# Pairs on diagonal strips, updates on two row strips, and the samples' queries as stationary column strips

## The chip, the cores and the metric

The kernel runs on one core of one Trainium2 chip. The metric is the device time of one execution in microseconds (us), as the median of several runs.

## The reference

One step of a recurrent decoder trunk: 256 prompt tokens and 8 samples of 4 tokens, 288 in all, width 2048. One normalised input goes through a large projection to five branches, each with its own gate; each branch is projected back, weighted by a sigmoid gate from the same input, summed and projected once more. Two branches are of one kind, and the change touches them alone: HGRN2 (8 heads, keys 128, values 128) and GLA (4 heads, keys 128, values 256). Per head, with a running sum b of log decays in chunks of 64 tokens:

```python
b = jnp.cumsum(gi, axis=2)
inter = jnp.einsum("nhtk,nhkv->nhtv", qi * jnp.exp(b), S)
decay = jnp.where(mask, jnp.exp(jnp.where(mask, diff, 0.0)), 0.0)
att = jnp.einsum("nhtk,nhsk,nhtsk->nhts", qi, ki, decay)
intra = jnp.einsum("nhts,nhsv->nhtv", att, vi)
S_new = jnp.exp(b_last)[..., None] * S + jnp.einsum("nhsk,nhsv->nhkv", ki * jnp.exp(b_last[:, :, None] - b), vi)
```

The prompt starts from a zero state; each of the 8 samples has a state S of its own per head, loaded from HBM, used by its 4 tokens and written back renewed.

## The kernel before

Weights stream in 522 units of 512 KB through four slots. SyncE issues each load when the slot's last unit was split; ACT rounds a unit to `w_hi` (fp32r), DVE subtracts to get `w_lo`, and PE does three matmuls per 128x128 block (hi*hi, lo*hi, hi*lo), 288 columns of tokens each, in `project`. A projection from the model width has two units and 48 matmuls, a branch's own projection (`branch`) one unit and 24. The order of all this is written out by hand: the list `ORDER`, and on ACT and DVE calls `upto(n)`, which process the units up to n in the engine's own queue. All work between the projections stands in the same queues. Each engine runs its list in order.

The stages touched run from about 560 to 1400 us: four GLA heads, then eight HGRN heads. The attention matrix of 128 tokens is built by levels: `HALVES` 64, 32, 16, ..., 1. For level l the distances of the decay to the middle of each block of 2h tokens stand in `g_X[:, l]`; after the exponentials on ACT (`distances`) DVE multiplies them with queries in the right half and keys in the left (`keys_and_queries`). Then PE multiplies `g_X[:, l]` with itself over 128 tokens (`pairs`), once for each level and once keys by queries for the diagonal, into two banks of PSUM (2 and 3). DVE masks the eight slices (`levels`) and sums them (`attention`). This is done for tokens 0 to 127 in `first_pairs`, for 128 to 255 in `second_pairs`, which waits for DVE to free the banks, a projection later. `first_pairs` also makes the samples' own 32x32 products (three, as only levels 2 and 1 and the diagonal lie within 4 tokens), the product between the two halves of the prompt, and the turned keys (`g_kT`). `end_keys_and_queries` gives the queries times exp(b) in the slot `CROSS` and signals `g_X`.

`mixed` sums, for a block of 128 values: attention times values, and for each of the 8 samples the whole state (128x128) as stationary operand with that sample's 4 query columns moving. `updates` makes what is added to the samples' states: turned keys of the 32 sample tokens (`g_kT[0:TS, 2]`) times the values, laid out by DVE (`own_values`) so that each sample has columns of its own, two products of 512 columns into banks 5 and 6; `new_states` adds them. GLA calls it twice a head (half 0 and 1), HGRN once, after the next head's forget projection and its `sum_squares`.

PE's order in an HGRN head is: hf, sum_squares and updates of the head before, hq, hi, gate C, turn_values, hg, first_pairs, gate C, second_pairs, two branch projections, mixed. In a GLA head: decay product, ck, cq, cv, cv, turn_values, gate D, first_pairs, cg, second_pairs, cg, mixed (values 0), branch, mixed (values 1), gate, updates, branch, sum_squares, gate, updates, and the rest of the gates and branches. GpSimd loads a head's states (`g_S0_landed`) when the stores of the head before have ended. The memory attention (`kc`, `eq_own`) and the S5 branch already use 32-wide strips of PE's array: an output on 32 partitions at 32j, with a stationary operand of 32 columns.

## Time and profile before

| | us |
|---|---|
| median of 3 runs | 2012.35 (2010.4 to 2014.06) |
| the profiled execution | 2009.41 |
| its span | 2007.7 |
| PE busy | 1949.1 |
| DVE busy | 1275.2 |
| ACT busy | 903.4 |
| POOL (GpSimd) busy | 414.1 |
| mean granted TensorE clock | 0.992 |

The span is the time from the first to the last instruction in one execution taken by the hardware profiler. PE is the matmul part of TensorE; an instruction's duration there is from its start to the end of its results, and consecutive ones overlap, so distances between starts say what one costs. One fp32 product shows as two matmul records, an fp32r one or a transpose as one. All helpers of one kind have one line (L1615 for matmuls), so groups are told apart by the names of their tiles. "ps" is PSUM.

### The profile page before, as it was taken

To read this page: it belongs to the slowest core of one execution; us is meant where nothing else is said; L and a number is where in the kernel's file an instruction comes from. 1 tells how busy PE (TensorE), PEld (TensorE's weight loads), DVE (VectorE), ACT (ScalarE), POOL (GpSimd) and SP (SyncE) were. 2 spreads that over 40 slices of the span, in tenths; PEclk is the share of its full clock that TensorE was granted. 3 is DMA by queue.
4 is the path that set the end of the run, shared out by engine and by line. 5 is a ranking of instruction groups with operands and counts; after the bars stand their busy time and mean duration, and the time that the engine had idled before them with its cause. 6 is when DMAs were issued, how large, how long until landed. Compare 5 with 4: busy or idle time off the path is not lost.

```text
span 2007.7 us, 37182 instructions
## 1 busy us (share of the span) xinstructions
PE 1949.1 (97%) x15518; PEld 1875.7 (93%) x15518; DVE 1275.2 (64%) x2106; ACT 903.4 (45%) x1307; POOL 414.1 (21%) x704
## 2 busy tenths in 40 slices
PE   6999999999999999999999999999999999999996
PEld 5999998999999999999999999999999999999996
DVE  8555467776575766666778777777565565544544
ACT  5543444544444344435455555454333333434442
POOL 5687778787000000000000000000000000000000
PEclk9999999999999999999999999999999999999998
DMA  7777664445444353535434344444555444454542
GB/s 269 279 280 257 236 216 163 168 171 182 164 155 174 136 180 126 186 122 185 146 138 170 130 157 138 149 148 144 205 186 191 170 154 156 171 198 158 177 160 90
DMA packets 91512, 350.50 MB, mean 175 GB/s; under 512 B 11760, under 2 KB 12160, under 8 KB 87760
## 3 DMA queue, kind: packets, MB, share of 16 engines
q1 hardware_dynamic: 76896, 280.53, 40.6%
q0 software_dynamic: 11568, 47.50, 6.6%
q10 hardware_dynamic: 2880, 20.09, 2.6%
q8 instruction: 123, 2.02, 0.4%
q14 instruction: 45, 0.37, 0.1%
HBM read 321.15 MB, written 26.92 MB: 173 GB/s over the span
## 4 chain that ended last, share of the span: by engine, by line
PE 59%; DVE 7%; ACT 4%; issue 3%; DMA 0%; POOL 0%; ACTq 0%; DVEq 0%
PE ps L1615 58%; DVE w_lo L1041 2%; DVE g_X L1035 2%; DVE g_X L1041 1%; ACT g_t L569 1%; ACT L569 1%; ACT w_hi L569 1%; DVE g_X L1044 0%; ACT g_X L569 0%; DVE g_b L1470 0%; PE ps L1922 0%; DVE acc L1038 0%; DMA a_h<-in_a_h 0%; DVE acc L1035 0%; DVE g_k L1041 0%
## 5 line engine op out<-in xcount | busy, mean ns | idle before, releaser
L1615 PE MATMUL ps<-h_hi,w_hi 128*128 128x288 f32 x2960 | 890.8, 301 | 18.7 <-ACT gate_t L569 7.3
L1041 DVE TENSOR_TENSOR w_lo<-raw,w_hi 128x1024 fp32r<-128x1024 f32 x522 | 650.8, 1258 | 393.3 <-ACT w_hi L569 389.9
L1615 PE MATMUL ps<-h_hi,w_lo 128*128 128x288 f32 x2960 | 877.1, 296 | 0.0
L1615 PE MATMUL ps<-h_lo,w_hi 128*128 128x288 f32 x2960 | 872.5, 295 | 3.0 <-DVE h_lo L1041 3.0
L569 ACT ACTIVATE w_hi<-raw 128x1024 fp32r<-128x1024 f32 x522 | 546.5, 1055 | 540.7 <-PE ps L1615 523.2
L1615 PEld LDWEIGHTS ps<-h_hi,w_hi 128*128 128x128 f32 x2960 | 559.3, 189 | 36.1 <-issue 17.8
L1615 PEld LDWEIGHTS ps<-h_lo,w_hi 128*128 128x128 f32 x2960 | 559.8, 189 | 3.6 <-DVE h_lo L1041 3.6
L1615 PEld LDWEIGHTS ps<-h_hi,w_lo 128*128 128x128 f32 x2960 | 560.2, 189 | 0.8
L1615 PE MATMUL ps<-br_hi,w_hi 128*128 128x288 f32 x640 | 193.1, 302 | 1.6 <-DVE d_gate L1047 1.6
L1615 PE MATMUL ps<-br_lo,w_hi 128*128 128x288 f32 x640 | 189.7, 296 | 0.0
L1615 PE MATMUL ps<-br_hi,w_lo 128*128 128x288 f32 x640 | 189.5, 296 | 0.0
L1615 PEld LDWEIGHTS ps<-br_hi,w_hi 128*128 128x128 f32 x640 | 120.9, 189 | 10.3 <-issue 7.3
L1615 PEld LDWEIGHTS ps<-br_hi,w_lo 128*128 128x128 f32 x640 | 120.4, 188 | 0.1
L1615 PEld LDWEIGHTS ps<-br_lo,w_hi 128*128 128x128 f32 x640 | 120.1, 188 | 0.0
L569 ACT ACT_TABLE_LOAD x85 | 109.1, 1283 | 4.9 <-PE ps L1615 2.6
L344 POOL DMA_DIRECT2D out_hg_s<-h_S x8 | 4.3, 532 | 439.1 <-DVE h_S L1047 439.1
L569 ACT ACTIVATE gate_t<-ps 128x288 f32<-128x288 f32 x80 | 32.3, 404 | 137.6 <-PE ps L1615 137.3
L1615 PE MATMUL ps<-o_hi,w_lo 128*128 128x288 f32 x256 | 76.6, 299 | 0.0
L1615 PE MATMUL ps<-o_lo,w_hi 128*128 128x288 f32 x256 | 76.1, 297 | 0.0
L1615 PE MATMUL ps<-o_hi,w_hi 128*128 128x288 f32 x256 | 75.7, 296 | 0.0
L344 POOL DMA_DIRECT2D out_gla_s<-c_S x4 | 2.1, 534 | 356.3 <-DVE c_S L1047 356.3
L1615 PE MATMUL ps<-m_hi,w_hi 128*128 128x256 f32 x256 | 72.3, 283 | 0.5 <-DVE gate_t L1047 0.3
(371 smaller groups left out, 2409.4 us busy)
## 6 DMA issues: line engine op xcount, KB each, us to landing
raw<-in_w SPq DMA_DIRECT2D x522, 512.0 KB, 3.8
w_scratch<-st_wide POOLq DMA_DIRECT2D x72, 128.0 KB, 3.5
a_w<-w_scratch POOLq DMA_DIRECT2D x8, 1152.0 KB, 8.1
acc<-in_kc ACTq DMA_DIRECT2D x4, 2048.0 KB, 7.9
vc<-in_vc ACTq DMA_DIRECT2D x4, 2048.0 KB, 10.1
c_S<-in_gla POOLq DMA_DIRECT2D x4, 1024.0 KB, 7.2
out_gla_s<-c_S POOLq DMA_DIRECT2D x4, 1024.0 KB, 5.1
h_S<-in_hgrn POOLq DMA_DIRECT2D x8, 512.0 KB, 3.9
```

The costliest lines, as they stand in the source:

```text
L344: pool.dma_start(dst, src).then_inc(S(name), 16)
L569: act.activation(out, in_, func, **kw).then_inc(sem if not isinstance(sem, str) else S(sem), 1)
L1035: return dve.tensor_tensor(out, a, b, ALU.mult)
L1041: return dve.tensor_tensor(out, a, b, ALU.subtract)
L1615: return pe.matmul(out, a, b, start=start, stop=stop)
```

## The change

- Pairs: for levels 16 to 1 and the diagonal only the 32x32 blocks on the diagonal of the 128 tokens are multiplied, four blocks on four column strips (bank 2); levels 64 and 32 multiply only the blocks that are not masked, four products ("far", bank 3). Both halves of the prompt are done in one `all_pairs`; `second_pairs` goes.
- Samples' states: the 4 queries of each sample stand in 32 columns of a cleared tile `g_own` and are the stationary operand on a column strip; the state moves through (`ps[:, 7]`, in `all_pairs`). ACT copies the results to `of_states`; `mixed` adds them by two products of 16 columns with columns of the identity. The wait for the loaded states moves from `mixed` to `all_pairs`.
- Updates: samples 0 to 3 stay on rows 0 to 15, samples 4 to 7 get rows 64 to 79; the two products of 512 columns have 16 rows each on two row strips. For this the keys and values of samples 4 to 7 are turned by an added product with the identity each and copied by ACT.
- DVE's `attention` masks and sums 2 x 192 columns, spreads the sums over the strips and copies the far blocks. Masks are prepared on GpSimd.

```diff
-        g_vm = g_prod[0:TS].rearrange("p l t -> p (l t)")
+        g_vm = g_prod[:].rearrange("p l t -> p (l t)")[:, 0:512]
+
+        def of_states(nv):
+
+            return g_prod[:].rearrange("p l t -> p (l t)")[:, 512:512 + 2 * nv * P].rearrange("p (h c) -> p h c", h=2)
+
+        halves_of_samples = (slice(0, 16), slice(64, 80))
+        g_own = sb("g_own", [P, NB, 32], F32, g_st)
...
+        near = levels[:, 1058:1250].rearrange("p (l t) -> p l t", t=32)
+        strips = levels[:, 1250:1254]
+        in_strip = levels[:, 1254:1258]
+        in_strip2 = levels[:, 1258:1262]
...
-            for mask, width, pattern in ((in_group[:], 16, [[-16, 8]]), (in_half[:, 0], 64, [[-64, 2]]),
-                                         (in_seq[:], NT, [[-NT, NB]])):
+            for mask, width, pattern, first in ((in_group[:], 16, [[-16, 8]], 0), (in_half[:, 0], 64, [[-64, 2]], 0),
+                                                (in_strip, NT, [[-NT, 4]], 0), (in_strip2, NT, [[-NT, 4]], 64)):
                 link(pool.memset(mask, 1.0))
-                for base, sign in ((0, 1), (width - 1, -1)):
...
+            by_strip = lev_mask[:, 2:8, :].rearrange("p l (s t) -> p l s t", s=4)
+            link(tt(ALU.add, near, by_strip[:, :, 0], by_strip[:, :, 1]))
+            for n in (2, 3):
+                link(tt(ALU.add, near, near, by_strip[:, :, n]))
+            link(tt(ALU.add, in_strip, in_strip, in_strip2))
+            link(tt(ALU.add, strips, in_group[:, 0:8:2], in_group[:, 1:8:2]))
             link(pool.memset(eq_own[:], 0.0))
...
+            pool.memset(g_own[:], 0.0).then_inc(S("g_own_clear"), 1)
...
+                f(vals[2][64:80, 2], ps[64:80, 4, 0:nv * P], ACT.Copy, "g_vT")
...
+                f(of_states(nv), ps[:, 7, 0:2 * nv * P].rearrange("p (h c) -> p h c", h=2), ACT.Copy, "g_of_states")
                 f(g_kT[:, 0:2], ps[:, 5, 0:2 * P].rearrange("p (a b) -> p a b", a=2), ACT.Copy, "g_kT")
                 f(g_kT[0:TS, 2], ps[0:TS, 5, 2 * P:3 * P], ACT.Copy, "g_kT")
+                f(g_kT[64:80, 2], ps[64:80, 5, 2 * P:3 * P], ACT.Copy, "g_kT")
...
-                mul(cross[:, P:T], cross[:, P:T], g_q[:, P:T])
+                mul(cross[:, P:SEQ], cross[:, P:SEQ], g_q[:, P:SEQ])
+                dve.wait_ge(S("g_own_clear"), 1)
+                mul(g_own[:, :, 0:NT], by_seq(cross), by_seq(g_q))
                 sg(mul(final, final, g_k[:]), "g_X")

-            def attention(i, nv, n):
+            def attention(i, nv):
                 w, _ = heads_of(i, nv)
-                w("levels", 3, 1 + 2 * n)
-                link(mul(g_prod[:].rearrange("p l t -> p (l t)"), ps[:, 2:4].rearrange("p a t -> p (a t)"),
-                         levels[:, 0:1024]))
-                sg(dve.tensor_reduce(g_att[:, 2 * n], g_prod[:].rearrange("p l t -> p t l"), AX.X, ALU.add), "g_att")
-                w("att", 3, 1 + 2 * n)
-                if n == 0:
-                    w("levels", 3, 2)
-                    own = g_prod[0:TS, 0:3, 0:TS]
-                    link(mul(own, ps[0:TS, 4, 0:3 * TS].rearrange("p (l t) -> p l t", t=TS), lev_mask[0:TS, 5:8, 0:TS]))
-                    sg(dve.tensor_reduce(g_atts[:], own.rearrange("p l t -> p t l"), AX.X, ALU.add), "g_att")
-                    w("att", 3, 2)
+                w("levels")
+                flat = g_prod[:].rearrange("p l t -> p (l t)")
+                prod = flat[:, 0:384].rearrange("p (a l t) -> p a l t", a=2, l=6)
+                summed = flat[:, 384:448].rearrange("p (a t) -> p a t", a=2)
+                own = flat[0:TS, 0:96].rearrange("p (l t) -> p l t", t=TS)
+                far = ps[:, 3, 0:SEQ].rearrange("p (a t) -> p a t", a=2)
+                att = g_att[:, 0:3:2]
+                for a in range(2):
+                    ins = mul(prod[:, a], ps[:, 2, 192 * a:192 * a + 192].rearrange("p (l t) -> p l t", t=32), near)
+                link(ins)
+                link(dve.tensor_reduce(summed, prod.rearrange("p a l t -> p a t l"), AX.X, ALU.add))
+                for a in range(2):
+                    ins = mul(att[:, a].rearrange("p (s t) -> p s t", s=4), summed[:, a:a + 1].to_broadcast([P, 4, 32]),
+                              strips.unsqueeze(2).to_broadcast([P, 4, 32]))
+                link(ins)
+                link(mul(own, ps[0:TS, 4, 0:3 * TS].rearrange("p (l t) -> p l t", t=TS), near[0:TS, 3:6]))
+                dve.tensor_reduce(g_atts[:], own.rearrange("p l t -> p t l"), AX.X, ALU.add)
+                for rows, cols in ((slice(0, 64), slice(64, 128)), (slice(0, 32), slice(32, 64)), (slice(64, 96), slice(96, 128))):
+                    ins = dve.tensor_copy(att[rows, :, cols], far[rows, :, cols])
+                sg(ins, "g_att")
+                w("att")
...
             def own_values(i, nv, vals, half):
                 w, wv = heads_of(i, nv)
-                n = NB // nv
+                n = 4 // nv
                 if half:
                     wv("up", half)
                 else:
-                    w("vT", 3, 3)
-                sg(mul(g_vm.rearrange("p (b v) -> p b v", v=nv * P),
-                       vals[2][0:TS, 2].unsqueeze(1).to_broadcast([TS, n, nv * P]),
-                       in_seq[:, half * n:(half + 1) * n].unsqueeze(2).to_broadcast([TS, n, nv * P])), "g_vm")
+                    w("vT", 4, 4)
+                for rows in halves_of_samples:
+                    ins = mul(g_vm[rows].rearrange("p (b v) -> p b v", v=nv * P),
+                              vals[2][rows, 2].unsqueeze(1).to_broadcast([16, n, nv * P]),
+                              in_strip[rows, half * n:(half + 1) * n].unsqueeze(2).to_broadcast([16, n, nv * P]))
+                sg(ins, "g_vm")
...
                     w("o")
-                for b in range(n):
-                    s = vals[0][:, half * n + b]
-                    ins = stt(s, s, g_eb[:, half * n + b:half * n + b + 1], up[:, b * nv * P:(b + 1) * nv * P],
-                              ALU.mult, ALU.add)
+                for j in range(2):
+                    for b in range(n):
+                        of = 4 * j + half * n + b
+                        s = vals[0][:, of]
+                        ins = stt(s, s, g_eb[:, of:of + 1], ps[:, 5 + j, b * nv * P:(b + 1) * nv * P], ALU.mult, ALU.add)
                 sg(ins, "g_new" if half == nv - 1 else "g_half_new")
...
-                attention(i, 2, 0)
+                attention(i, 2)
-                attention(i, 2, 1)
...
-                attention(i, 1, 0)
-                upto(u0 + 13)
-                attention(i, 1, 1)
+                attention(i, 1)
...
                         pe.transpose(ps[:, 2 + tt, v * P:(v + 1) * P], vals[1][:, v, tt * P:(tt + 1) * P], ident[:])
-                    ins = pe.transpose(ps[0:TS, 4, v * P:(v + 1) * P], vals[1][:, v, SEQ:T], ident[:])
+                    pe.transpose(ps[0:TS, 4, v * P:(v + 1) * P], vals[1][:, v, SEQ:T], ident[:])
+                for v in range(nv):
+                    ins = mm(ps[64:80, 4, v * P:(v + 1) * P], vals[1][:, v, SEQ + 16:T], ident[:])
                 sg(ins, "g_vt")

-            lev = ps[:, 2:4].rearrange("p a (l t) -> p (a l) t", t=P)
-
             def pairs(tok):
-                for l in range(7):
-                    mm(lev[:, l], g_X[:, l, tok], g_X[:, l, tok])
-                sg(mm(lev[:, DIAG], g_k[:, tok], g_q[:, tok]), "g_levels")
-
-            def first_pairs(i, nv):
+
+                at_ = tok // P * 192
+                for n in range(6):
+                    for j in range(4):
+                        c = slice(tok + 32 * j, tok + 32 * j + 32)
+                        x, y = (g_X[:, n + 2, c], g_X[:, n + 2, c]) if n < 5 else (g_k[:, c], g_q[:, c])
+                        mm(ps[32 * j:32 * j + 32, 2, at_ + 32 * n:at_ + 32 * n + 32], x, y)
+
+                for l, j, first, width in ((0, 0, 64, 64), (0, 1, 64, 64), (1, 0, 32, 32), (1, 2, 96, 32)):
+                    mm(ps[32 * j:32 * j + 32, 3, tok + first:tok + first + width],
+                       g_X[:, l, tok + 32 * j:tok + 32 * j + 32], g_X[:, l, tok + first:tok + first + width])
+
+            def all_pairs(i, nv, vals):
                 w, _ = heads_of(i, nv)
                 w("X")
-                w("vT", 3, 3)
-                pairs(slice(0, P))
+                w("vT", 4, 4)
+                pairs(0)
+                pairs(P)
+                n, _ = heads_before(i, nv)
+                pe.wait_ge(S("g_S0_landed"), n * 16 + 16)
+                for half in range(2):
+                    for j in range(4):
+                        b = 4 * half + j
+                        mm(ps[32 * j:32 * j + 32, 7, half * nv * P:(half + 1) * nv * P], g_own[:, b], vals[0][:, b])
                 for n, (a, b) in enumerate(((g_X[:, 5], g_X[:, 5]), (g_X[:, 6], g_X[:, 6]), (g_k, g_q))):
                     ins = mm(ps[0:TS, 4, n * TS:(n + 1) * TS], a[:, SEQ:T], b[:, SEQ:T])
                 sg(ins, "g_levels")
                 mm(ps[:, 6, 0:P], g_X[:, CROSS, 0:P], g_X[:, CROSS, P:2 * P])
                 for tt in range(2):
                     pe.transpose(ps[:, 5, tt * P:(tt + 1) * P], g_X[:, FINAL, tt * P:(tt + 1) * P], ident[:])
-                sg(pe.transpose(ps[0:TS, 5, 2 * P:3 * P], g_X[:, FINAL, SEQ:T], ident[:]), "g_kt")
-
-            def second_pairs(i, nv):
-                w, _ = heads_of(i, nv)
-                w("att", 3, 1)
-                pairs(slice(P, 2 * P))
+                pe.transpose(ps[0:TS, 5, 2 * P:3 * P], g_X[:, FINAL, SEQ:T], ident[:])
+                sg(mm(ps[64:80, 5, 2 * P:3 * P], g_X[:, FINAL, SEQ + 16:T], ident[:]), "g_kt")

             def mixed(i, nv, vals, v):
                 w, _ = heads_of(i, nv)
-                n, _ = heads_before(i, nv)
                 if v == 0:
-                    w("att", 3, 3)
+                    w("att")
                     w("cross_out")
-                    pe.wait_ge(S("g_S0_landed"), n * 16 + 16)
+                    w("of_states")
+                own = ident[:].rearrange("p (j r) -> p j r", r=32)[:, :, 0:NT]
                 out, val = ps[:, 2 + v], lambda m: vals[2][:, m, v * P:(v + 1) * P]
                 mm(out[:, 0:2 * P], val(0), g_att[:, 0:2].rearrange("p a t -> p (a t)"), True, False)
                 mm(out[:, P:2 * P], val(1), g_att[:, 2], False, False)
                 mm(out[:, SEQ:T], val(2)[0:TS], g_atts[:], False, False)
-                for b in range(NB):
-                    seq = slice(SEQ + b * NT, SEQ + (b + 1) * NT)
-                    ins = mm(out[:, seq], vals[0][:, b, v * P:(v + 1) * P], g_X[:, CROSS, seq], False, b == NB - 1)
+                for half in range(2):
+                    ins = mm(out[:, SEQ + 16 * half:SEQ + 16 * half + 16], of_states(nv)[:, half, v * P:(v + 1) * P], own,
+                             False, half == 1)
...
-                w("kT", 2, 2)
+                w("kT", 3, 3)
...
                 wv("vm", half + 1)
                 if half:
                     pe.wait_ge(S("g_half_new"), i + 1)
-                mm(ps[:, 5], g_kT[0:TS, 2], g_vm[:, 0:512])
-                sg(mm(ps[:, 6], g_kT[0:TS, 2], g_vm[:, 512:1024]), "g_up")
+                for j, rows in enumerate(halves_of_samples):
+                    ins = mm(ps[:, 5 + j], g_kT[rows, 2], g_vm[rows])
+                sg(ins, "g_up")
...
-                first_pairs(i, 2)
+                all_pairs(i, 2, c_values)
                 h("cg", 2 * i)
-                second_pairs(i, 2)
...
-                first_pairs(i, 1)
+                all_pairs(i, 1, h_values)
                 gate("C", 2 * i + 1)
-                second_pairs(i, 1)
```

## Rows read from the trace of the kernel before

**Rows 1.** The page, part 1: busy us by engine, share of span, instructions

```profile
PE 1949.1 (97%) x15518; PEld 1875.7 (93%) x15518; DVE 1275.2 (64%) x2106; ACT 903.4 (45%) x1307; POOL 414.1 (21%) x704
```

**Rows 2.** Who PE waited for: total us, times, longest us

```profile
PE ps L1615 <- DVE w_lo L1041: 4.3, 8, 0.6
PE ps L1615 <- DVE g_X L1035: 3.1, 7, 0.5
```

**Rows 3.** PE, third HGRN head: start us, duration us, instruction, count [idle before]

```profile
1079.55 1.83 PE L1615 MATMUL ps<-g_X 128*128 128x128 f32 x14 [0.44 <-DVE g_X L1035]
1081.53 0.31 PE L1615 MATMUL ps<-g_X 128*32 128x32 f32 x4
1081.68 0.23 PE L1615 MATMUL ps<-g_q,g_k 128*32 128x32 f32 x2
1081.84 0.49 PE L1615 MATMUL ps<-g_X 128*128 128x128 f32 x2
1082.41 0.38 PE L1615 MATMUL ps<-h_hi,w_hi 128*128 128x288 f32 x1
```

**Rows 4.** The same view, the second block of pairs of that head

```profile
1088.89 1.77 PE L1615 MATMUL ps<-g_X 128*128 128x128 f32 x14
1090.64 0.38 PE L1615 MATMUL ps<-br_hi,w_hi 128*128 128x288 f32 x1
```

**Rows 5.** PE timeline with four column strips: memory attention, S5 branch

```profile
72.09 1.93 PE L1615 MATMUL ps<-acc,eq_own 128*32 128x256 f32 x32
73.95 0.38 PE L1615 MATMUL ps<-m_hi,w_hi 128*128 128x256 f32 x1
...
1401.88 0.64 PE L1615 MATMUL ps<-a_w 128*32 128x128 f32 x16
1402.45 0.40 PE L1615 MATMUL ps<-h_hi,w_hi 128*128 128x288 f32 x1
...
1429.99 1.21 PE L1615 MATMUL ps<-a_H,a_w 128*32 128x72 f32 x64
1431.13 0.40 PE L1615 MATMUL ps<-br_hi,w_hi 128*128 128x288 f32 x1
```

**Rows 6.** PE's timeline, the mixed block of the third HGRN head

```profile
1098.19 1.95 PE L1615 MATMUL ps<-g_X,h_S 128*128 128x4 f32 x16
1099.99 0.69 PE L1615 MATMUL ps<-h_vT,g_kT 128*128 128x128 f32 x4
```

**Rows 7.** PE's timeline, products of 16 columns in the memory attention

```profile
110.31 0.96 PE L1615 MATMUL ps<-ident,prob 128*128 128x16 f32 x8
111.12 0.36 PE L1615 MATMUL ps<-m_hi,w_hi 128*128 128x256 f32 x1
```

**Rows 8.** PE's timeline, updates of the first GLA head

```profile
616.34 1.98 PE L1615 MATMUL ps<-g_prod,g_kT 32*128 32x512 f32 x4
618.25 0.40 PE L1615 MATMUL ps<-br_hi,w_hi 128*128 128x288 f32 x1
```

**Rows 9.** ACT, DVE and PE, third HGRN head; last line: before S5

```profile
1050.15 0.50 ACT L569 ACTIVATE g_t<-ps,eps 128x288 f32<-128x288 f32 x1 [5.31 <-PE ps L1615]
...
1063.56 1.23 DVE L1041 TENSOR_TENSOR w_lo<-raw,w_hi 128x1024 fp32r<-128x1024 f32 x1 [2.00 <-ACT w_hi L569]
1079.04 0.45 DVE L1035 TENSOR_TENSOR g_X<-g_X,g_k 128x288 f32<-128x288 f32 x1
...
1068.93 0.40 PE L1615 MATMUL ps<-h_hi,w_hi 128*128 128x288 f32 x1 [0.57 <-DVE w_lo L1041]
...
1400.88 0.52 PE L1922 MATMUL ps<-ident,a_w 128*128 128x128 f32 x3 [0.54 <-issue]
```

**Rows 10.** GpSimd's timeline: the load of a head's states

```profile
1060.92 0.53 POOL L344 DMA_DIRECT2D h_S<-in_hgrn  x1 [2.87 <-DMA out_hg_p<-h_Sp]
```

**Rows 11.** Stretches: length, busy us by engine, granted clock, DMA share, GB/s

```profile
983.80:987.20 3.40, 3.40 (x17) 3.40 (x16) 1.38 (x2) 1.84 (x3) 0.00 (x0) 0.50 0.75 243
1274.20:1277.50 3.30, 3.30 (x15) 3.30 (x16) 1.45 (x2) 1.95 (x3) 0.00 (x0) 0.52 0.77 236
```

More of the change, by code:

```diff
@@ L124, in build @@
         in_half = sb("in_half", [P, 2, 2])
-        in_seq = sb("in_seq", [TS, NB])
         norm_cols = sb("norm_cols", [P, 3, KT])
@@ L283, in build @@
         ps = ctx.enter_context(nc.psum_tensor("ps", [P, 8, 512], F32))
-        up = ps[:, 5:7].rearrange("p a c -> p (a c)")
         landed = [S(f"landed{s}") for s in range(SLOTS)]
@@ L374, in _ @@
                                     fill=1.0, base=0, pattern=[[-1, P]], channel_multiplier=1))
-            for mask, width, pattern in ((in_group[:], 16, [[-16, 8]]), (in_half[:, 0], 64, [[-64, 2]]),
-                                         (in_seq[:], NT, [[-NT, NB]])):
+            for mask, width, pattern, first in ((in_group[:], 16, [[-16, 8]], 0), (in_half[:, 0], 64, [[-64, 2]], 0),
+                                                (in_strip, NT, [[-NT, 4]], 0), (in_strip2, NT, [[-NT, 4]], 64)):
                 link(pool.memset(mask, 1.0))
-                for base, sign in ((0, 1), (width - 1, -1)):
+                for base, sign in ((-first, 1), (first + width - 1, -1)):
                     link(pool.affine_select(out=mask, in_=mask, compare_op=ALU.is_ge, fill=0.0, base=base,
                                             pattern=[[a * sign, b] for a, b in pattern], channel_multiplier=sign))
+            by_strip = lev_mask[:, 2:8, :].rearrange("p l (s t) -> p l s t", s=4)
[4 more added lines that the diff above has]
+            link(tt(ALU.add, strips, in_group[:, 0:8:2], in_group[:, 1:8:2]))
             link(pool.memset(eq_own[:], 0.0))
@@ L1349, in own_values @@
                 else:
-                    w("vT", 3, 3)
-                sg(mul(g_vm.rearrange("p (b v) -> p b v", v=nv * P),
-                       vals[2][0:TS, 2].unsqueeze(1).to_broadcast([TS, n, nv * P]),
-                       in_seq[:, half * n:(half + 1) * n].unsqueeze(2).to_broadcast([TS, n, nv * P])), "g_vm")
+                    w("vT", 4, 4)
[4 more added lines that the diff above has]
+                sg(ins, "g_vm")
             def new_states(i, nv, vals, half):
                 w, wv = heads_of(i, nv)
-                n = NB // nv
+                n = 4 // nv
                 wv("up", half + 1)
```

## The prediction

> **What bounds the kernel now.** I read the engine line of the page first: TensorE (PE) is busy 97% of the span, VectorE (DVE) 64%, ScalarE (ACT) 45% [rows 1]. A microsecond of PE work is therefore worth about a microsecond, unless PE then waits for somebody. So the second view was PE's waits. Whole-span waits are small, but two of them lie where the change works: weight units (w_lo) and g_X, the latter in seven heads [rows 2]. The third view is PE's timeline around one HGRN head. The page's mean duration of a matmul is a latency and useless for a sum: matmuls overlap. I cost by start-to-start distance. Each fp32 product is two matmul records.
>
> **Pairs, before.** In the HGRN head read here the first block starts at 1079.55 and the next projection at 1082.41: 2.86 us [rows 3]. The second block runs 1088.89 to 1090.64: 1.75 us [rows 4]. Together 4.6 us; 0.11 us per record of 128 columns.
>
> **Pairs, after.** Per head 48 products of 32x32 on four column strips, 8 "far" ones of 64 or 32 columns, 8 products with the states, the unchanged three products of the samples, cross and turned keys, and one extra product for the keys of samples 4 to 7.
> - The 48: do the strips overlap? Rows that have four column strips: 32 records of 256 columns in 1.86 us, 0.058 each, although 256 columns in turn would be twice 0.11; 16 records of 128 columns in 0.57; 64 records of 72 columns in 1.14 [rows 5]. So yes: a step of four strips costs what one strip costs. For 32 columns the nearest row is the samples' own products, all on one strip: four records in 0.15 us, 0.0375 [rows 3]. 96 records in 24 steps at 0.036 are 0.9 us. Lower bound: 0.028 a step (32/128 of 0.11), 0.7. Upper bound: the 72-column step, 1.14/16 = 0.07, 1.7. I take 0.9, as it has the right column count.
> - Far products: strip 0 does 64 and 32 columns, two records each, about 0.18 per token half, 0.35 in all (0.7 if nothing overlaps).
> - States: four steps. HGRN 128 columns: 0.57; GLA 256 columns: half of 1.86 = 0.93 [rows 5].
> - The samples' three products 0.31, cross and transposes 0.57, as now (1081.53, 1081.84, 1082.41) [rows 3].
> - Extra key product: two records, 0.22, and about 0.1 for the change of shape: 0.3. Entry 0.1.
> Sum: HGRN 3.1 us against 4.6, **1.5 to 1.6 saved**; GLA 3.45, 1.2 saved. With the upper step and no overlap of the far ones the saving is 0.5 to 0.8 less.
>
> **Mixed.** Now every block of values has eight products of 4 columns with a whole state as stationary: 16 records, 1098.19 to 1099.99, 1.80 us [rows 6]. After: two products of 16 columns, four records. The nearest row is the 16-column product with the same strided identity, 8 records in 0.81, 0.10 to 0.11 each [rows 7]; four are 0.45. **1.35 saved**, once in an HGRN head, twice (2.7) in a GLA head.
>
> **Updates.** Two products of 512 columns take 1.91 us (616.34 to 618.25) [rows 8]. On two row strips with two banks they should overlap: 0.95 to 1.05. The trace shows no two-strip case; bounds are no overlap (0) and full overlap (0.95). I take 0.85 saved per call.
>
> **Turning values.** One more fp32 product per block of values on strip 64: two records of 0.11 and a change of shape, 0.25 to 0.5. GLA costs 0.5 a head.
>
> **Where PE's gain is eaten: the HGRN chain.** In heads 1 to 7 PE issues the sum of squares after the forget projection, then the updates, then three projections, the turn, one more projection, then the pairs. From the sum of squares ACT and DVE run one serial chain: ACT reads it at 1050.15 (it had idled 5.31 us for it), DVE's w_lo at 1063.56 waits for ACT, and the last g_X product starts at 1079.04 [rows 9]. PE waits for this chain 0.57 us at 1068.93 [rows 9] and 0.44 at the pairs [rows 3]. A shorter updates block is inside that stretch, as is the longer turn, so both only change PE's waiting: **the 0.85 is lost in seven HGRN heads**, and I count the turn at nothing. If that cover were gone the turn would cost 0.25 to 0.5 a head. After the eighth head the S5 preparation already waits (0.54 at 1400.88) [rows 9] on the same kind of chain, so 0.85 is lost there too. The chain gets one more small DVE product (g_own), 0.1 us a head: that is paid.
>
> **Other edits.** DVE's attention shrinks from two passes over 1024 columns to one over 384 plus small copies; it lies beside projections and starts earlier. ACT gets a copy of 256 or 512 columns and two or three small ones per head, before its next weight unit; PE has four slots of units, and ACT is busy 45% [rows 1]. In the queues: DVE's wait for "levels" now ends after the states' products, some 1.5 us later; behind it stand two weight units that PE needs a projection later. PE's wait for the loaded states moves from mixed to the pairs, with everything of PE behind it: the load is issued at 1060.92 and pairs start at 1079.55 [rows 3, 10], so it has over 15 us. GpSimd's extra mask work (some 3 us at the start) and its clear of g_own come long before their users. Nothing for these; bound 0.3 us a head if a weight unit is late.
>
> **Clock.** Three times in the HGRN heads the granted clock falls to 0.5 for 3.4 us, the first at 983.8, the last at 1274.2 [rows 11], each time right behind a mixed block with its 16 records of 4 columns. That is the lower level, 1.2 GHz; a fall costs about 1.5 us. With the mixed block 1.35 shorter and denser I expect all three to go: 4.5 us. The bounds are none of it and all of it.
>
> **Sum.** GLA: 1.2 + 2.7 + 1.7 - 0.5 = 5.1 a head, times 4 = 20.4. HGRN: 1.6 + 1.35 - 0.1 = 2.85, times 8 = 22.8. Clock 4.5. Together 47.7 us. The profiled execution took 2009.4 (span 2007.7): 1961.7. The median of the runs is 2.9 us higher, 2012.35; I carry part of that and say **1964 us**, 2.4% faster.
>
> **A rule that speaks against it.** The small products are short of columns already. The 72-column row gives 0.018 us per record [rows 5], with strips overlapped. The Trainium skill, page "TensorEngine Tiling (Array Packing)", section "Instruction Overhead", says that each matmul carries about 60 cycles whatever its width and that a tiling factor should not be taken from a dimension that is already small. An estimate from that page, 60 cycles at 2.4 GHz or 25 ns for each of 96 records, one after the other, would be 2.4 us a head instead of 0.9 and the time 1982; by the row at 0.018 the overhead does not add up over strips.
>
> **Rivals.**
> - A, the forecast: 1964. Chance 0.60.
> - B, small terms at their bad ends: steps of four at 0.07 (0.8 us a head, 12 heads: +9.5), or the clock still falls (+4.5), or row strips don't overlap (eight GLA calls, +6.8). One or two of these: 1969 to 1979. Chance 0.20. For it: a 32-column step of four strips stands nowhere in the trace.
> - C, the HGRN chain gives way, because part of it is tied to PE's progress: the updates' 0.85 comes back in eight heads, 1957. Chance 0.09. Against it: PE stalls twice in that stretch [rows 3, 9], so the chain is late there and not PE.
> - D, narrow records don't overlap: 96 records at 0.0375 are 3.6 us a head, 2.7 more, 33 us in all: 1997. Chance 0.06.
> - E, the other side: no column strip overlaps here, as strips wait in turn for their 128-row moving operand. D's 33, the states at 16 records of 0.11 (HGRN +1.2, times 8) or twice that (GLA +2.5, times 4), the far ones +4, the updates +6.8: 63 us more, 2027, slower than before. It decides from about 4 us a head more than forecast, which is an average record of the pairs over 0.05. Against it stand all three rows of strips [rows 5]. Chance 0.03.
> - The rest, 0.02, is a wait nobody sees here.
>
> **How the numbers follow.** A, B and C hold 0.89; leaving out their outer ends gives 1954 to 1979 for 8 in 10. A measurement of this kernel can tell some 0.2%, 4 us. Faster 0.96 (A to D), same 0.01, slower 0.03.
>
> **What would show it.** Right: a pairs block of 3.1 us (HGRN) and 3.4 to 3.5 (GLA) with no second block; groups of 16 columns in 0.45; updates in 1.05; in heads 1 to 7 PE's wait for w_lo near 1.4 us and g_X as before, so head-to-head distance shorter by 2.9 to 3.0, not by 3.8; no half clock in the HGRN heads. Wrong: pairs above 4 us (D); updates still 1.9 (B); waits for w_lo unchanged with shorter updates (C); PE waiting on ACT for g_of_states or on the states' load.

## The result and the profile after

| | before | after |
|---|---|---|
| median, us | 2012.02 (4 runs) | 1967.3 (4 runs, 1966.72 to 1967.86) |
| ratio, 95% interval | | 0.9777 (0.976 to 0.9794) |
| profiled execution, us | 2009.41 | 1967.86 |
| its span | 2007.7 | 1966.1 |
| PE busy | 1949.1 | 1901.9 |
| mean granted clock | 0.992 | 0.993 |

The kernel is 2.2% faster; 1964 us, 2.4%, was forecast. On one profiled execution the span fell by 41.6 us, where the sum had 47.7. In what follows an HGRN head is the distance from one head's projection to the same one of the next, and a clock fall is a stretch of 3.4 us (or two) at half clock.

The page of after, part 1, as [rows 1]:

```profile
PE 1901.9 (97%) x16534; PEld 1826.0 (93%) x16534; DVE 1239.7 (63%) x2182; ACT 919.1 (47%) x1343; POOL 422.7 (22%) x713
```

Who PE waited for in after (total us, times, longest), as [rows 2]:

```profile
PE ps L1647 <- DVE w_lo L1061: 9.9, 15, 0.8
...
PE ps L1964 <- issue: 1.4, 1, 1.4
```

PE's share is what it was. Its waits for w_lo went from 4.3 to 9.9 us, the g_X ones are gone, and the wait ahead of S5 grew from 0.54 to 1.4. That is the HGRN chain holding harder.

PE's timeline of after in HGRN heads (start, duration, instruction, count, [idle before]): the two waits of a head, the turn of the values, the pairs block, mixed, and the sum of squares with the updates.

```profile
1044.96 0.37 PE L1647 MATMUL ps<-h_hi,w_hi 128*128 128x288 f32 x1 [0.77 <-DVE w_lo L1061]
...
1048.96 0.40 PE L1647 MATMUL ps<-h_hi,w_hi 128*128 128x288 f32 x1 [0.58 <-DVE w_lo L1061]
...
1052.27 0.38 PE L1818 MATMUL ps<-ident,h_v 128*128 128x128 f32 x2
1052.48 0.27 PE L1819 MATMUL ps<-ident,h_v 128*32 128x128 f32 x1
1052.69 0.39 PE L1647 MATMUL ps<-ident,h_v 128*16 128x128 f32 x2
1053.01 0.40 PE L1647 MATMUL ps<-h_hi,w_hi 128*128 128x288 f32 x1
...
1059.65 0.53 PE L1647 MATMUL ps<-g_X 128*32 128x32 f32 x38
1059.99 0.21 PE L1647 MATMUL ps<-g_q,g_k 128*32 128x32 f32 x1
...
1060.10 0.65 PE L1647 MATMUL ps<-g_X 128*32 128x32 f32 x44
...
1060.82 0.60 PE L1647 MATMUL ps<-h_S,g_own 128*32 128x128 f32 x13
...
1062.29 0.39 PE L1647 MATMUL ps<-ident,g_X 128*16 128x128 f32 x2
1062.61 0.40 PE L1647 MATMUL ps<-h_hi,w_hi 128*128 128x288 f32 x1
...
1076.59 0.62 PE L1647 MATMUL ps<-ident,g_prod 128*128 128x16 f32 x4
1077.05 0.69 PE L1647 MATMUL ps<-h_vT,g_kT 128*128 128x128 f32 x4
...
1083.97 0.65 PE L1647 MATMUL ps<-h_o,ones 128*128 128x288 f32 x2
1084.55 1.13 PE L1647 MATMUL ps<-g_prod,g_kT 16*128 16x512 f32 x4
1085.61 0.40 PE L1647 MATMUL ps<-h_hi,w_hi 128*128 128x288 f32 x1
```

One pairs block, 1059.65 to 1062.61 or 2.96 us, stands for the 2.86 and 1.75 of [rows 3] and [rows 4]. The four records of 16 columns take 0.46 instead of the 1.80 of [rows 6], the updates 1.06 instead of the 1.91 of [rows 8].

Head to head, in heads without a clock fall:

| us a head | before | after | gain | forecast |
|---|---|---|---|---|
| GLA (4) | 95.56 | 90.91 | 4.65 | 5.1 |
| HGRN (8) | 57.48 | 54.49 | 3.0 | 2.85 |

These make 42.6 us. The three falls of before in these stages [rows 11] are gone, 4.2 us by the heads with one (58.6, 59.0 and 59.0) and without one (57.5): 46.8 us in the two stages, of 47.7 forecast. Another 0.6 us came behind them. But the first GLA head starts its turn of values at 581.22 instead of 575.38. **5.8 us were lost where the forecast counted nothing**, in the stages before the heads.

### The profile page after: what moved, and what is told of

Read it like the earlier page. It is cut to its first block, busy times and chain, and to the rows that moved or that the text cites. A ratio compares the mean times of both kernels' runs of the same rounds, so it can differ in the third digit from the quotient of the medians.

```text
span 1966.1 us, 39310 instructions
## 1 busy us (share of the span) xinstructions
PE 1901.9 (97%) x16534; PEld 1826.0 (93%) x16534; DVE 1239.7 (63%) x2182; ACT 919.1 (47%) x1343; POOL 422.7 (22%) x713
## 4 chain that ended last, share of the span: by engine, by line
PE 63%; DVE 4%; ACT 3%; issue 2%; DMA 0%; POOL 0%; ACTq 0%; DVEq 0%
PE ps L1647 62%; DVE w_lo L1061 2%; ACT g_t L586 1%; ACT L586 1%; ACT w_hi L586 1%; DVE g_X L1061 1%; PE ps L1964 0%; DVE acc L1058 0%; DVE g_b L1504 0%; DVE acc L1055 0%; DMA a_h<-in_a_h 0%; PE ps L1818 0%; DMA out_hg_p<-h_Sp 0%; DVE g_k L1061 0%; ACT g_k L586 0%
## 5 line engine op out<-in xcount | busy, mean ns | idle before, releaser
L1647 PEld LDWEIGHTS ps<-br_hi,w_hi 128*128 128x128 f32 x640 | 119.9, 187 | 10.3 <-issue 7.3
```

Of the source, the lines that this page charges most:

```text
L1647: return pe.matmul(out, a, b, start=start, stop=stop)
```

## Where the 5.8 us lie

Three things, from the distances between the same projection matmuls in both traces: 1.0 us at 22 to 27 us; 2.5 us between 57 and 250 us; and the rest, 2.3 us, which goes with clock falls that lie elsewhere (after at 27.6 and 338.2, 6.8 us each; before at 314.8 and 505.9, 3.4 each).

VectorE's timeline of after at the start, GpSimd's of the same time, and VectorE's of e2, where the masks' additions come later:

```profile
22.36 2.41 DVE L1067 SCALAR_TENSOR_TENSOR acc<-acc,norm_cols,rstd 128x288 f32<-128x288 f32 x4
24.68 1.67 DVE L1061 TENSOR_TENSOR h_lo<-acc,h_hi 128x1152 fp32r<-128x1152 f32 x1
```

```profile
22.99 3.43 POOL L356 TENSOR_TENSOR levels<-levels 128x192 f32<-128x192 f32 x4
...
25.22 1.20 POOL L356 TENSOR_TENSOR levels<-levels 128x4 f32<-128x4 f32 x1
26.50 0.35 POOL L356 TENSOR_TENSOR levels<-in_group 128x4 f32<-128x4 f32 x1
```

```profile
22.34 1.79 DVE L1067 SCALAR_TENSOR_TENSOR acc<-acc,norm_cols,rstd 128x288 f32<-128x288 f32 x4
24.05 1.34 DVE L1061 TENSOR_TENSOR h_lo<-acc,h_hi 128x1152 fp32r<-128x1152 f32 x1
```

The first GpSimd row holds four additions, of which the last is the second row: three of 192 columns (0.75, 0.62 and 0.62 us) and one of 4 columns.

While GpSimd runs the mask additions, VectorE's four products take 2.41 instead of 1.79 us and the subtraction 1.67 instead of 1.35, and PE waits for h_lo. Page "SBUF — State Buffer" of the Trainium skill, section "SBUF: two separate sides", says that VectorE (when it has two inputs in SBUF) and GpSimd (when it reads SBUF) share one pair of ports, that the one which starts first holds it for its whole instruction and that the other is blocked until then. The rows agree: each of VectorE's operations that starts after one of the long additions grows, two products from 0.50 to 0.85 and 0.78 and the subtraction by 0.32, each by less than what is left of that addition; the product that had started before the first addition keeps its 0.50. The addition of 4 columns, which starts behind the subtraction, ends with it, after 1.20 us instead of the 0.35 of the next one.

The memory attention's 256-column matmuls (`m_hi`, `m_lo`) have nothing to do with the change. First and last start of one run of 144 on PE's timeline, in after and then in e1:

```profile
231.56 0.36 PE L1647 MATMUL ps<-m_hi,w_hi 128*128 128x256 f32 x1
...
248.80 0.28 PE L1647 MATMUL ps<-m_lo,w_hi 128*128 128x256 f32 x1
```

```profile
228.99 0.36 PE L1648 MATMUL ps<-m_hi,w_hi 128*128 128x256 f32 x1
...
245.76 0.28 PE L1648 MATMUL ps<-m_lo,w_hi 128*128 128x256 f32 x1
```

143 distances: 17.24 us or 120.6 ns each in after, 16.77 or 117.3 in e1. The mean distance without the pauses between weight units is 120.0 and 116.7; 768 such matmuls make 2.5 us. What differs is where the tiles lie in SBUF: the diff takes out `in_seq`, 32 bytes a partition, and every tile allocated later moves down by 32.

## Experiments: the early loss

**e1.** Give the 32 bytes back.

```diff
         in_half = sb("in_half", [P, 2, 2])
+        gap = sb("gap", [P, NB])
         norm_cols = sb("norm_cols", [P, 3, KT])
```

> The changed kernel with one unused tile of 32 bytes a partition where in_seq was, so that every tile allocated after it lies at its old address. Theory (addresses): the change took 32 bytes out of the allocation, and in 72 to 300 us, where nothing of the change runs, the 256-column matmuls of the m projections went from 116.7 ns apart to 119.95 ns; 768 of them make 2.5 us. With the gap back they return to 116.7 ns, the o projections from 133.3 to about 134.4 ns, and the time falls by 1.5 to 2.5 us, to 1965 to 1966 us. Rival (the spacing has to do with the new instructions or with the clock): 120 ns stays, and the time with it, at 1967.3 us.

1964.14 us, ratio 0.9753 (0.9727 to 0.9779). The m matmuls are 116.9 ns apart (116.7 before the change), the o matmuls go up from 133.3 to 134.4. Both as the theory says. The address, not the new work, set the spacing. The total fell by 3.2 us; its interval overlaps that of after, so the verdict rests on the spacing, which is 116.7 to 116.9 ns, as the mean of a kernel, in all five kernels profiled here with m at its old place and h untouched, and 119.9 to 120.0 in all seven with m 32 bytes lower.

**e2.** The five additions later.

```diff
-            link(tt(ALU.add, near, by_strip[:, :, 0], by_strip[:, :, 1]))
...
             pool.wait_ge(S("d_stored"), 32)
+            link(tt(ALU.add, near, by_strip[:, :, 0], by_strip[:, :, 1]))
...
             pool.memset(g_own[:], 0.0).then_inc(S("g_own_clear"), 1)
```

> The changed kernel with GpSimd's five additions that build the four-strip masks moved from the first 26 us to the place before g_own is cleared, which is after the first stage. Theory (they slow VectorE): the additions lie beside VectorE's first operations, which grew from 0.50 to 0.8 us (the product that accumulates) and from 1.35 to 1.67 us (h_lo's subtraction); without them TensorE's first projection starts 1.0 us earlier, for 1966.3 us, and if the clock's fall at 27.6 us was a result of that delay it goes too, another 1.3 us, for 1965 us. Rival (VectorE's growth has another cause): 1967.3 us and the fall at 27.6 us as before.

1965.72 us, 0.9759 (0.9735 to 0.9784). VectorE's operations are back at 1.79 and 1.34 (above) and the first 32 projection matmuls take 9.94 us instead of 10.88, so the mechanism is shown and its price is 0.95 us. The clock fall did not go: it came at 30.4, and another at 409.3. The falls of the first 550 us are not set by this change's work: kernels with the same code up to there reached the first GLA heads with 3.4 to 20.5 us of half clock in them, and their 3400th projection matmul came between 536.5 and 544.5 us. What sets them stays open.

## Experiments: what the HGRN chain holds

**e3.** Sum of squares of the last head between the halves of `hf`, so that ScalarE's and VectorE's chain starts earlier.

```diff
-                h("hf", i)
-                if i:
-                    sum_squares(i - 1, 1, h_values)
+                project(("hf", i), h_hi, h_lo, between=(lambda: sum_squares(i - 1, 1, h_values)) if i else None)
+                if i:
```

> The changed kernel with the last head's sum of squares issued between the two halves of the hf projection instead of behind it (HGRN only); nothing is left out. Theory (the chain ScalarE square, VectorE h_y, VectorE w_lo is what TensorE waits for in HGRN heads): the chain begins about 3 us earlier, TensorE's waits for w_lo (9.9 us over 15) go in seven heads, and w_lo's 1.35 us a head come back, less whatever ends next: 6 to 9 us, 1958 to 1961 us. Rival A (the chain begins with TensorE's own work and the wait only moves to another step): under 2 us. Rival B (the earlier square waits behind ScalarE's own queue and puts later evictions off): slower by up to 3 us.

1954.77 us, 0.9709 (0.9676 to 0.9743): 12.5 us less than after, more than forecast. The waits for w_lo fall from 9.9 us, in 15 waits, to one wait of 0.3:

```profile
PE ps L1647 <- DVE w_lo L1061: 0.3, 1, 0.3
```

The head goes from 54.49 to 52.58. I had summed the shown waits, 0.77 + 0.58 = 1.35; the two weight units that end in them shrink, start to start, from 4.13 and 4.00 to 3.20 each, 1.73. The view counts idle time from the end of the last matmul's record, which is 0.29 us long, while the next matmul would have started 0.13 us after it: most of the missing 0.16 to 0.22 us a wait lies there.

**e5 and e8.** Both update products on one row strip, in the changed kernel and in e3. This is the forecast's own claim, that the updates' 0.85 us is used in GLA and lost in HGRN.

```diff
-                    ins = mm(ps[:, 5 + j], g_kT[rows, 2], g_vm[rows])
+                    ins = mm(ps[:, 5 + j], g_kT[0:16, 2], g_vm[0:16])
```

> The changed kernel with both update products of a call taken from rows 0 to 15, so that they lie on one row strip and follow each other; samples 4 to 7 thereby get the keys and values of samples 0 to 3, and their states and outputs are not the reference's. The count and shapes of the instructions stay. Theory (prediction: the updates' gain is used in GLA and lost in the HGRN heads behind ScalarE's and VectorE's chain): each call grows by 0.85 us, two calls a GLA head are 8 x 1.7 = 13.6 us, and in HGRN 8 x 0.85 = 6.8 us would be added but TensorE's wait for w_lo shrinks by as much only if the chain does not begin with the updates' end; the chain does begin there, so HGRN gets +6.8 too only if the sum of squares is late by it. Numbers: the chain begins with the sum of squares on the updates' second half; theory 'lost' +13.6 us, 1981 us; rival 'all on the path' +20.4 us, 1988 us; rival 'strips never overlapped' 0, 1967 us.

> The kernel of e3 (sum of squares between the halves of hf) with both update products of a call on one row strip, as in e5 (samples 4 to 7 get the keys and values of samples 0 to 3, so their results are not the reference's). e5 showed the overlap of the two row strips worth 0.85 us a call in GLA (four heads, two calls each: 6.8 us) and nothing in the eight HGRN heads. Theory (the chain from the sum of squares hides it in HGRN): with the chain out of the way the HGRN heads pay too, 8 x 0.85 = 6.8 us, so this is 13.6 us above e3, 1968.4 us, and the HGRN head's period goes from 52.58 to 53.4 us. Rival (HGRN hides it for another reason): 6.8 us above e3, 1961.6 us, period 52.6 us.

e5 took 1976.41 us (0.982, 0.9798 to 0.9841), 9.1 over after (single executions 1973.9 to 1979.8), e8 1967.79 (0.9775, 0.9755 to 0.9794), 13.0 over e3. e5's expectation counts eight GLA heads; there are four, so "lost" means 6.8 and "all on the path" 13.6. The heads decide it better than the medians:

| us a head | squares behind hf | squares in the middle |
|---|---|---|
| updates on two strips | 54.49 (after) | 52.58 (e3) |
| updates on one strip | 54.47 (e5) | 53.42 (e8) |

With the chain in place 0.85 us of PE work more or less changes nothing; with it out of the way the same work costs 0.84. Behind the eighth head it is covered even then: the wait ahead of S5 is 1.38 us in e3 and 0.52 in e8. GLA heads pay either way: 90.91 to 92.59, 1.68. The updates of a GLA head, on one strip (e5) and on two (after), with the instruction behind each:

```profile
803.84 1.98 PE L1647 MATMUL ps<-g_prod,g_kT 16*128 16x512 f32 x4
805.75 0.40 PE L1647 MATMUL ps<-br_hi,w_hi 128*128 128x288 f32 x1
```

```profile
801.05 1.13 PE L1647 MATMUL ps<-g_prod,g_kT 16*128 16x512 f32 x4
802.11 0.40 PE L1647 MATMUL ps<-br_hi,w_hi 128*128 128x288 f32 x1
```

1.91 against 1.06 with the same four records: two row strips overlap almost wholly.

**e11.** The kernel before with e3's edit alone.

> The kernel before with only the sum of squares moved between the halves of hf. In it TensorE waits 0.57 us for w_lo at the head's first reload [rows 9] and less often elsewhere: 4.3 us over 8 waits, and 0.54 ahead of S5. Theory (the chain bounds the HGRN heads before the change too, by less, since the slower updates covered 0.85 us of it): 0.6 to 1.1 us a head, 5 to 8 us, 2004 to 2007 us, so the change's own worth counted with the chain out of the way on both sides is 2005.5 - 1954.8 = 51 us instead of 45. Rival (the chain's hold is of the change's making): 2012 us.

2004.72 us, 0.9963 (0.995 to 0.9977). The head without a clock fall goes from 57.46 to 55.72, 1.74, more than expected, so the chain held before the change too. In the profiled execution clock falls ate part of it: five lengths of 3.4 us in the HGRN heads instead of the three of before. With the chain out on both sides the change is worth 2004.7 - 1954.8 = 50 us instead of 45, and 55.72 - 52.58 = 3.14 in the head.

## Experiments: the strips and the states

**e6.** All 48 small products on column strip 0.

```diff
-                        mm(ps[32 * j:32 * j + 32, 2, at_ + 32 * n:at_ + 32 * n + 32], x, y)
+                        mm(ps[0:32, 2, at_ + 32 * n:at_ + 32 * n + 32], x, y)
```

> The changed kernel with the 48 products of 32x32 of a head all written to column strip 0 (partitions 0 to 31) instead of one in four on each strip; count and shape of the instructions stay, the pairs' attention is left wrong. This prices the overlap of column strips. Theory (four strips share a step of 32 ns, as the after trace shows): on one strip each product takes its own 32 ns or more, 48 x (32 - 8) = 1.15 us a head in one record each, 2.3 us if both records of an fp32 product count: +2.3 us a head in GLA, and in HGRN, where the pairs lie before the chain's start, as well: +37 us, 2004 us. Rival D of the prediction (narrow records do not overlap): no change, 1967 us. With one record a product: +18 us, 1985 us.

1993.44 us, 0.9906 (0.9883 to 0.9929), 26.1 over after. Here too the expectation's total counts too many GLA heads; 2.3 us a head over twelve is 27.6. Heads: HGRN +2.24, GLA +2.24. PE's timeline of e6, pairs:

```profile
1078.82 1.45 PE L1647 MATMUL ps<-g_X 128*32 128x32 f32 x40
1080.11 0.39 PE L1647 MATMUL ps<-g_q,g_k 128*32 128x32 f32 x7
```

40 records in 1.29 us, 0.032 each, on one strip. In after 38 such records take 1059.65 to 1059.99, 0.036 for a step of four (0.034 if the 40 of the program are counted, as two records are missing). The overlap of four column strips at 32 columns is practically complete. Without it the change of the pairs would be a loss: 2.96 + 2.24 = 5.2 us in an HGRN head against 4.6 before.

About the rule weighed in the prediction, of the Trainium skill's page "TensorEngine Tiling (Array Packing)", section "Instruction Overhead": four instructions on four strips take what one takes on one strip, so an overhead of each instruction does not add up over strips. How large it is these runs don't show. The steps of 256, 128 and 72 columns in [rows 5] cost 0.9 to 1.1 ns a column, and 32 columns at that price are already 0.03 us.

**e4.** The states stationary again.

```diff
-                for half in range(2):
-                    ins = mm(out[:, SEQ + 16 * half:SEQ + 16 * half + 16], of_states(nv)[:, half, v * P:(v + 1) * P], own,
+                for b in range(NB):
+                    seq = slice(SEQ + b * NT, SEQ + (b + 1) * NT)
+                    ins = mm(out[:, seq], vals[0][:, b, v * P:(v + 1) * P], g_own[:, b, 0:NT], False, b == NB - 1)
```

> The changed kernel with the third part of the change undone: the samples' states are stationary again (8 loads of 128 columns and 4 moving columns a values block, in fp32), and the products through four column strips with their copy on ScalarE are gone. Theory (as the prediction costed it): the mixed block goes from 1.99 back to about 3.3 us in HGRN (+1.35) and by twice that in GLA, and the turning block ahead of it gives back its 0.5 in HGRN and 0.74 in GLA, so +0.85 and +1.95 us a head, 8 heads each: +22 us with nothing hidden, to 1990 us, and up to 4.5 us more if the clock's falls return. Rival (HGRN heads wait for ScalarE's and VectorE's chain, so that more TensorE time there is hidden in it): HGRN +0, GLA +1.95 a head, +16 us, 1983 us.

1993.1 us, 0.9897 (0.9874 to 0.9921), 25.8 over after. Both counts were wrong, and with four GLA heads they were 14.6 and 7.8, so the miss is larger. A head without a fall: HGRN 54.49 to 55.37, +0.9, all of it paid (it lies behind the end of the chain). GLA, by blocks: mixed +1.34 twice, pairs -0.87, the turn unchanged, since its added product belongs to the values and not to the states: +1.8. Work: 8 x 0.9 + 4 x 1.8 = 14.3. The rest is clock: the GLA and HGRN stages have ten lengths of 3.4 us at half clock where after has none, at about 1.5 us each (heads of 56.9 against 55.4 us) 15 us. This execution was 2.3 us quicker before these stages, and 2.4 us came back behind them, between 1382 and 1406, where the wait of 1.4 us ahead of S5 is missing in e4. That sums to 24.6; the two profiled executions lie 24.7 apart, the medians 25.8. Two of the stretches (length, busy us of PE, its weight loads, DVE, ACT, POOL, granted clock, DMA share, GB/s):

```profile
794.80:798.10 3.30, 3.30 (x16) 3.30 (x15) 0.61 (x1) 0.00 (x0) 0.00 (x0) 0.50 0.48 150
801.60:804.90 3.30, 3.30 (x12) 2.93 (x12) 0.20 (x1) 2.02 (x4) 0.00 (x0) 0.50 0.00 0
```

Blocks of 16 records of 4 columns end at 793.7 and 801.4, just ahead of the two; 0.50 is the level of 1.2 GHz. Over all profiles the pattern holds: the three kernels with 4-column products (before, e4, e11) have 3, 10 and 5 such lengths in these stages, the eleven others one in all (e7, at 1333.9). So about half of what lies between e4 and after is clock, not work. Why e4 has ten and before three isn't settled.

## Experiments: a better version

**e7** puts e1, e2 and e3 together.

> The changed kernel with the gap of 32 bytes, the masks' additions later and the sum of squares between the halves of hf, all three. Theory: their gains add, since they lie in different stages (72 to 300 us, the first 35 us, the HGRN heads): -2, -1 to -2.3 and -6 to -9 us, 1954 to 1958 us. Rival (one of them is what its own rival says): the sum without it; if the sum of squares brings nothing, 1963 us.

1952.68 us, 0.9693 (0.9673 to 0.9714): 14.6 us below after, where the three gains taken singly add up to 17.3 (3.2, 1.6 and 12.5). The intervals allow that; the 2.1 us to e3 alone are within the spread of single executions.

**e9** puts the gap only ahead of `m_hi`, **e10** adds 64 bytes ahead of `h_hi`, **e12** moves m once more.

```diff
+        gap_h = sb("gap_h", [P, 16])
         h_hi = sb("h_hi", [P, KT, T], F32R)
...
+        gap = sb("gap", [P, 24], F32, e_st)
         m_hi = sb("m_hi", [P, KT, N_MEM], F32R, e_st)
```

(That is e12; e9 has no `gap_h` and 8 for 24, e10 has 8 for 24.)

> The kernel of e7 (masks later, squares between the halves) with the 32-byte gap moved from where in_seq was to right before m_hi, so that the m tiles lie 32 bytes past a multiple of 128 as before the change, and the o and branch tiles stay on multiples of 128. Theory (each tile's own address sets its matmul's spacing): m 116.7 ns as in e1, o 133.3 ns as in the changed kernel instead of 134.4, the branches' 1920 matmuls a few tenths of ns less: 0.9 to 1.3 us below e7, 1951.5 us. Rival (the gap must lie early, it is norm_cols or another small tile that matters): m 120 ns, 2.5 us above e7, 1955 us.

> The kernel of e9 with 64 unused bytes ahead of h_hi, so that h, branch and o tiles lie 64 bytes past a multiple of 128 and the m tiles 96. It asks whether the 288-column matmuls, which take 133 ns on multiples of 128 and 133.4 to 134.4 ns at 32, have a cheaper place as the 256-column ones have (120 to 116.7 ns). Theory (only a place 32 or 96 bytes off a multiple of 64 changes the spacing): 133.0 ns for h, m at 116.7, the time of e9 within 1 us. Rival (64 is a place of its own): a gain or loss of up to 3 ns on each of 12000 matmuls, up to 36 us either way.

> The kernel of e10 with the m tiles 64 bytes further, 32 bytes past a multiple of 128 (in e10 they lay at 96, and their matmuls took 120 ns, against 116.8 at 32 in e7 and e9); h, branches and o stay at 64, where their 288-column matmuls took 132.0 ns instead of 133.1. Theory (each tile's place by itself): m 116.7 ns, h 132.0 ns, and 768 x 3.2 = 2.5 us less than e10, 1941.3 us. Rival (m's place counts against that of h, not by itself): m stays at 120 ns, 1943.8 us.

| | us | ratio, interval | h, 288 columns | m, 256 columns | o, 288 |
|---|---|---|---|---|---|
| after | 1967.3 | 0.9777 (0.976 to 0.9794) | at 0: 133.2 ns | at 0: 120.0 | at 0: 133.3 |
| e7 | 1952.68 | 0.9693 (0.9673 to 0.9714) | 0: 133.2 | 32: 116.7 | 32: 134.4 |
| e9 | 1953.93 | 0.9711 (0.9692 to 0.9731) | 0: 133.3 | 32: 116.9 | 0: 133.3 |
| e10 | 1943.78 | 0.966 (0.9643 to 0.9677) | 64: 132.2 | 96: 120.0 | 64: 132.2 |
| e12 | 1940.72 | 0.9648 (0.9624 to 0.9672) | 64: 132.2 | 32: 117.7 | 64: 132.2 |

h, m and o are the tiles that are the moving operand; h stands for the input of most projections. The places are bytes past a multiple of 128, the spacings means over the consecutive matmuls of a tile, without distances over 150 ns and without half clock. e9: m and o as the theory says, but worth too little to show in the median. e10: the theory fell, the rival held. A place at 64 brings 1 ns on each of some 12,000 matmuls and takes 2.5 us back on m, 10 us below e9. For 288 columns the place alone does not settle the spacing at 32: with o, z and the branches' tiles all there (before, e1, e7) o takes 134.4 ns, but z 133.3 and the branches 133.3 to 133.4, where they take 133.3 and 133.2 at 0. Windows of 60 us of PE late in the kernel, where little but projections runs, in after and then in e10 (columns as above):

```profile
1700.00:1760.00 60.00, 60.00 (x452) 60.00 (x451) 30.60 (x41) 24.82 (x36) 0.54 (x1) 1.00 0.58 192
```

```profile
1700.00:1760.00 60.00, 60.00 (x456) 60.00 (x455) 29.58 (x38) 22.20 (x31) 0.00 (x0) 1.00 0.53 176
```

452 matmuls against 456. e12 gets m back to 117.7 (not quite 116.7) and has the lowest median here: 3.5% faster than before, 26.6 us below the changed kernel. Its single executions (1939.3 to 1948.3) overlap those of e10, so that it is the better of the two rests on the spacing. Why the places differ isn't known; only four of them were tried, 96 with m alone and 64 with the 288-column tiles alone.

## Why the prediction was right, and where it was not

- **Bound and method.** Right: counted by PE's starts, the heads came out within 0.45 and 0.15 us of what was measured.
- **Pairs.** HGRN 3.1 forecast, 2.96 measured; a step of four strips 0.036 forecast, 0.034 to 0.036 measured. GLA's block takes 3.39 us (589.15 to 592.54), at the edge of the forecast 3.4 to 3.5, but counted with the slower restarts on both sides of a block the gain is 1.03 and not 1.2: -0.7 us in all.
- **Mixed.** 1.34 measured, 1.35 forecast. In an HGRN head this and the pairs' 1.65 are already the 3.0 that were measured, so the 0.1 us counted for g_own doesn't show.
- **Updates.** 0.85 as taken, and lost in the HGRN heads: the step with the least support in the trace of before, shown by e5 and e8. The forecast wait of about 1.4 us came as 1.35. That PE would wait for g_X as before was wrong: this wait is gone, and the longer turn, which stands ahead of it on PE, most likely took its place.
- **Turning values.** GLA 0.5 forecast, 0.74 measured, 1.0 us in all. The four records of 16 columns take 0.54, and 0.20 go by before they start, where in before the projection followed after 0.03:

```profile
581.82 0.27 PE L1819 MATMUL ps<-ident,c_v 128*32 128x128 f32 x1
582.02 0.61 PE L1647 MATMUL ps<-ident,c_v 128*16 128x128 f32 x4
582.56 0.40 PE L1647 MATMUL ps<-h_hi,w_hi 128*128 128x288 f32 x1
```

  The price of going from one mode of product to another was put at 0.1.
- **Clock.** Right in these stages: three falls gone, 4.2 us of the forecast 4.5.
- **The step that failed** is "GpSimd's extra mask work (some 3 us at the start) and its clear of g_own come long before their users. Nothing for these". It asked when the masks are needed and not what runs beside them: 0.95 us (e2). And the removal of `in_seq` was not costed at all: 2.5 us (e1). So the sum, 1961.7, missed the profiled execution of 1967.9 by 6.2 us. The forecast of 1964 is nearer by luck: it carried over part of the 2.9 us by which the median of before lay above its profiled execution, while the median of after lies 0.6 us below its own.
- **Rivals.** B's mechanisms did not occur; C, D and E fell: D and E by after's own step of 0.036 and by e6, where taking the overlap away costs 26 us; C by e5 and e8. The signs of a wait for `g_of_states` or for the states' load are absent from PE's waits in after.

## What to carry to other kernels

Before crediting a PE saving, ask which chain is behind it: a saving inside a stretch that another engine's chain bounds is lost until that chain is started earlier, and then both gains come together. Small products overlapped almost fully here on four column strips, down to 32 moving columns, and on two row strips at 512 columns, so pack them. After any edit to the allocations compare the spacing of the unchanged matmuls in both traces: moving the tiles by 64 bytes changed 12,000 of them by 1 ns, 10 us, where this whole change brought 45; moving one by 32 bytes changed 768 of them by 3 ns.

## What the runs showed of the hardware that was not expected

- Spacing of fp32r matmuls by the moving tile's place modulo 128 bytes: 256 columns 120.0 ns at 0 and 96, 116.7 to 117.7 at 32; 288 columns 133.2 to 133.3 at 0, 132.2 at 64, and at 32 134.4 for one tile (o) but 133.3 to 133.4 for two others.
- A shown wait of PE of 0.58 to 0.77 us lengthens the unit that ends in it by 0.80 to 0.93, as idle time is counted from the end of a record of 0.29 us and not from the next start, due after 0.13.
- At 22 to 27 us of after, where VectorE and GpSimd both read SBUF, the one that started later was held up by the other: VectorE's products of 0.50 us took 0.78 and 0.85 beside GpSimd's additions, and an addition of 4 columns took 1.20 beside VectorE's subtraction instead of 0.35.
- Half clock follows blocks of 4-column products: 3, 10 and 5 lengths in the GLA and HGRN stages of the three kernels that have them, one in all in the eleven that don't; the falls of the first 550 us come and go between executions of the same code.
